# Attention heads of block 1 with the values stationary: probabilities turned by products with diagonals of inverse row sums

## The reference

```python
def first_block(x, w_in, ..., w_out, norm_mix, norm_ffn, w_ff1, w_ff2):
    for l in range(DEPTH):
        h = rmsnorm(x, norm_mix[l])
        proj = jnp.einsum('bsd,de->bse', h, w_in[l])
        ...
        y_m = mlstm(qk[..., :M_WIDTH], qk[..., M_WIDTH:], m_v, m_o, ...)
        y_b = moba(b_q, b_k, b_v, ...)
        y_n = nsa(n_q, n_kc, n_vc, n_ks, n_vs, n_kw, n_vw, n_g, ...)
        mix = jnp.concatenate([y_m, y_b, y_n], axis=-1)
        x = x + jnp.einsum('bse,ed->bsd', mix, w_out[l])
        h = rmsnorm(x, norm_ffn[l])
        u = jnp.square(jax.nn.relu(jnp.einsum('bsd,df->bsf', h, w_ff1[l])))
        x = x + jnp.einsum('bsf,fd->bsd', u, w_ff2[l])
# in nsa, for each head:
    return gj[:, 0] * o_c + gj[:, 1] * o_s + gj[:, 2] * o_w
```

## Time and profile before

| | us |
|---|---|
| runs | 1138.59, 1140.25, 1141.14; median 1140.25 |
| the profiled execution | 1139.48 |
| its span | 1137.7 |
| TensorE busy | 1089.9 (96%) |
| VectorE busy | 717.2 (63%) |
| ScalarE busy | 623.3 (55%) |
| GpSimd busy | 57.5 (5%) |
| block 1, layer 0: projection and heads | about 11 to 170 |
| block 1, layer 1: the same | about 346 to 506 |

### The profile page before, as it was taken

How to read it: one execution, slowest core, us unless ns; L and a number is a source line. 1 busy time by engine, 2 the same in 40 slices (tenths; PEclk the granted TensorE clock), 3 DMA queues, 4 the chain that set the end, 5 groups by cost and what they waited for, 6 DMA issues and landing times.

```text
span 1137.7 us, 17472 instructions
## 1 busy us (share of the span) xinstructions
PE 1089.9 (96%) x6848; PEld 952.3 (84%) x6848; DVE 717.2 (63%) x1260; ACT 623.3 (55%) x983; POOL 57.5 (5%) x75
## 2 busy tenths in 40 slices
PE   8989989999999989899999999999999899999997
PEld 6878779899888977779998987798988677989885
DVE  4799577555557898576555556774445657844555
ACT  4555746445545555745454445665657447666562
POOL 0010000000000000100000000004000000040000
PEclk8999999999999999999999999999999999999999
DMA  8753336655666542346656655554453455444441
GB/s 272 236 162 94 111 111 209 198 186 186 185 190 206 181 130 87 118 128 206 187 187 183 195 187 185 168 152 131 120 158 118 129 161 168 149 130 131 147 130 56
DMA packets 89087, 181.17 MB, mean 159 GB/s; under 512 B 8797, under 2 KB 19933, under 8 KB 89005
## 3 DMA queue, kind: packets, MB, share of 16 engines
q1 hardware_dynamic: 87565, 175.79, 49.8%
q10 hardware_dynamic: 1440, 4.26, 1.1%
HBM read 178.98 MB, written 1.05 MB: 158 GB/s over the span
## 4 chain that ended last, share of the span: by engine, by line
PE 73%; DVE 14%; ACT 5%; issue 5%; DMA 2%; POOL 1%; SPq 0%; DVEq 0%; POOLq 0%; ACTq 0%
PE bank L778 21%; PE bank L780 21%; PE bank L779 21%; DVE w_lo L1623 4%; ACT w_hi L1252 2%; DMA raw<-in_w_in 2%; PE bank L855 2%; PE bank L906 1%; DVE xn L1895 1%; DVE vecs L1632 1%; PE bank L953 1%; PE bank L1191 1%; PE bank L962 1%; PE bank L963 1%; PE bank L929 1%
## 5 line engine op out<-in xcount | busy, mean ns | idle before, releaser
L1623 DVE TENSOR_TENSOR w_lo<-raw,w_hi 128x1024 fp32r<-128x1024 f32 (+1 forms) x320 | 389.4, 1220 | 309.2 <-ACT w_hi L1252 305.0
L1252 ACT ACTIVATE w_hi<-raw 128x1024 fp32r<-128x1024 f32 (+1 forms) x320 | 334.8, 1051 | 243.2 <-PE bank L780 219.6
L778 PE MATMUL bank<-h_hi,w_hi 128*128 128x256 f32 x896 | 257.4, 287 | 4.2 <-ACT hid_parts L1391 4.1
L780 PE MATMUL bank<-h_hi,w_lo 128*128 128x256 f32 x896 | 253.3, 283 | 0.0
L779 PE MATMUL bank<-h_lo,w_hi 128*128 128x256 f32 x896 | 253.3, 283 | 0.0
L778 PE MATMUL bank<-w_hi,h_hi 128*128 128x512 f32 (+1 forms) x448 | 182.6, 407 | 5.4 <-DVE h_lo L1642 4.8
L778 PEld LDWEIGHTS bank<-h_hi,w_hi 128*128 128x128 f32 x896 | 170.9, 191 | 8.2 <-issue 7.0
L780 PE MATMUL bank<-w_hi,h_lo 128*128 128x512 f32 (+1 forms) x448 | 176.4, 394 | 0.0
L779 PE MATMUL bank<-w_lo,h_hi 128*128 128x512 f32 (+1 forms) x448 | 176.2, 393 | 0.0
L779 PEld LDWEIGHTS bank<-h_lo,w_hi 128*128 128x128 f32 x896 | 171.0, 191 | 0.5
L780 PEld LDWEIGHTS bank<-h_hi,w_lo 128*128 128x128 f32 x896 | 170.9, 191 | 0.0
(11 more groups left out here) (290 smaller groups left out, 1329.2 us busy)
## 6 DMA issues: line engine op xcount, KB each, us to landing
raw<-in_w_in SPq DMA_DIRECT2D x144, 512.0 KB, 3.8
raw<-in_w_ff SPq DMA_DIRECT2D x128, 512.0 KB, 4.0
raw<-in_w_out SPq DMA_DIRECT2D x40, 512.0 KB, 3.2
raw<-in_w_in SPq DMA_DIRECT2D x8, 404.0 KB, 5.8
xn<-in_cmp_w SPq DMA_DIRECT2D x8, 256.0 KB, 5.0
x_sb<-in_x SPq DMA_DIRECT2D x2, 512.0 KB, 7.5
mix<-in_cmp_w SPq DMA_DIRECT2D x4, 256.0 KB, 4.7
gain<-in_cmp_w SPq DMA_DIRECT2D x4, 256.0 KB, 5.5
```

The lines of the kernel that those rows point to most:

```text
L778: pe.matmul(out_ap, s_hi, m_hi, start=start, stop=False, **kw)
L780: return pe.matmul(out_ap, s_lo, m_hi, start=False, stop=stop, **kw)
L1252: act.activation(slot(w_hi, u), slot(raw, u), ACT.Copy).then_inc(hi_ready, 1)
L1623: dve.tensor_tensor(slot(w_lo, u), slot(raw, u), slot(w_hi, u).bitcast(F32), ALU.subtract)\
```

## The change

The twelve heads go in six pairs, two heads from start to end (the nsa heads are listed so that a pair takes two heads of the same branch). Each pair gets a stage D on VectorE: reciprocals of its row sums, from head 4 on times the gate, and four 128x128 diagonals of these (row_scale, in the place of vecs). T is then a full product of a block of probabilities with a diagonal, which turns and scales at once. In V the values are stationary, 64 columns for each of two heads side by side, and the turned probabilities move (256 and 128 columns), so the result has features in the partitions. It is split directly into mixT_hi and mixT_lo (mix_rows). The epilogue, mix_turn 2 and 3 and the addition of cmp_o on VectorE go; cmp_o accumulates into the same bank. Some steps move: cmp 0 and 1 to p = 13 and 14, cmp_kT to 20, cmp_s and cmp_soft to 22, cmp_pT to 25, mLSTM scores 3 to 27 and values 3 to 28, ff_params with two casts to 29, three memsets to GpSimd at the start. mlstm_end goes in two halves of two heads each; its last two wide products become four products of 128x128 for each half. Banks change, and some one-element copies that served as signals are gone, since their readers wait for the bank's own semaphore.

```diff
-        start = [13, 14, 15, 16] + list(range(18, 26))
+        start = [13, 15, 18, 20, 22, 24]
         def heads1(p):
-            for stage, lag in (("V", 4), ("T", 2), ("E", 1), ("S", 0)):
+            name = ("att1", l)
+            for c, first in enumerate(start):
+                if first + (4 if c == 5 else 5) == p:
+                    if c in (0, 2):
+                        use((*name, "O", c // 2), 7)
+                    if c in (1, 5):
+                        done((*name, "O", c // 4))
+                    step(*name, "V", 2 * c)
+                    if c in (1, 5):
+                        step("mix_rows", l, c // 4)
+            for h in range(12):
+                c = h // 2
+                if start[c] + 3 + (h % 2 if c < 5 else 0) == p:
+                    use((*name, "T", h), 4 if h == 11 else 6)
+                    step(*name, "T", h)
+            for c, first in enumerate(start):
+                if first + 2 == p:
+                    step(*name, "D", 2 * c)
+            for stage, lag in (("E", 1), ("S", 0)):
                 for h in range(12):
...
+                    if start[h // 2] + lag == p:
+                        head_steps(name, h, stage, None)
...
+                if p == 22:
                     single(0, "cmp_s", l, 0)
                     single(1, "cmp_s", l, 1)
                     step("cmp_soft", l)
-                if p == 21:
-                    single(0, "mix_turn", 0, l, 2)
-                if p == 24:
+                if p == 25:
                     single(3, "cmp_pT", l)
-                if p == 25:
                     m_scores(0, 2)
                 if p == 26:
-                    single(3, "cmp_o", l)
+                    step("cmp_o", l)
...
             if p == 28:
-                m_scores(3, 4)
                 m_values(2, 5)
+                step("mlstm_end", l, 0, 0)
+                m_values(3, 4)
             if p == 29:
-                single(6, "mix_turn", 0, l, 3)
-                m_values(3, 5)
-                step("mlstm_end", l, 0)
+                step("mlstm_end", l, 0, 1)
+                step("mlstm_end", l, 1, 0)
+                if l == 0:
+                    step("ff_params")
             if p == 30:
-                step("mlstm_end", l, 1)
+                single(7, "mix_turn", 0, l, 0)
+                step("mlstm_end", l, 1, 1)
             if p == 31:
-                single(7, "mix_turn", 0, l, 0)
                 single(5, "mix_turn", 0, l, 1)
...
+            def value_pair(l, h):
+                for c in range(2):
+                    drained(pe, ("att1", l, "T", h + c))
+                group = ("att1", l, "O", h // 4 if h < 4 else 1)
...
+                for i in range(NT):
+                    for c in range(2):
+                        v = heads_of("att1", l)[h + c][3](i)
+                        weight = probsT_at("att1", h + c)
+                        mm = pe.matmul(ps[HD * c:HD * c + HD, lo + i * P:lo + T], v, weight[:, i * T:i * T + T - i * P],
+                                       start=first and i == 0, stop=last and i == 1, skip_group_check=True)
...
                     else:
-                        pe.wait_ge(exp_ready, nth_head(kind, l, h))
+                        pe.wait_ge(scale_ready, 6 * l + h // 2 + 1)
...
+                        if kind == "att1":
+                            mm = pe.matmul(ps[:, b * P:(b + 1) * P], block_, row_scale[h // 2 % 2][:, 2 * (h % 2) + (b + 1) // 2, :],
+                                           start=True, stop=True)
+                        else:
+                            mm = pe.transpose(ps[:, b * P:(b + 1) * P], block_, ident)
...
+                def scale_rows(h):
+                    dve.wait_ge(exp_ready, nth_head("att1", l, h + 1))
+                    inv = row_inv[:, 0:2, :]
+                    link(dve.reciprocal(inv, row_sum[:, h // 2 % 2, 0:2, :]))
+                    if h >= 4:
+                        n, branch = divmod(h - 4, 4)
+                        at_gate = 4 * (1 + branch // 2) + 2 * n
+                        tt(inv, inv, n_gate[:, :, at_gate:at_gate + 2].rearrange("p i h -> p h i"), ALU.mult)
+                    dve.tensor_tensor(row_scale[h // 2 % 2], ident.unsqueeze(1).broadcast_to([P, 4, P]),
+                                      inv.rearrange("p h i -> p (h i)").unsqueeze(2).broadcast_to([P, 4, P]), ALU.mult)\
+                        .then_inc(scale_ready, 1)
```

More of the change, by code:

```diff
@@ L296, in hybrid_blocks @@
                 if p == 16:
-                    single(3, "hidden", l)
+                    single(2, "hidden", l)
                 if p == 17:
                     single(3, "turn", l, 2)
-                    single(3, "turn", l, 3)
+                    single(2, "turn", l, 3)
                 if p == 18:
@@ L303, in hybrid_blocks @@
                     single(3, "turn", l, 5)
[L304 to L307, removed]
                 if p == 20:
+                    single(1, "cmp_kT", l)
+                if p == 22:
                     single(0, "cmp_s", l, 0)
@@ L582, in hybrid_blocks @@
         prm_rows = o_tmp[:, 0:2 * P]
+        row_scale = [vecs[:, 1536 * b:1536 * b + 512].rearrange("p (n t) -> p n t", t=P) for b in range(2)]
         ident = const[:, C_ID:C_ID + P]
@@ L1043, in _ @@
                             ps = open_bank(("hidden_parts", l))
-                            pe.wait_ge(blocks_ready, l + 1)
+                            drained(pe, ("turn", l, 4))
                         for a in range(16):
@@ L1417, in _ @@
                         softmax_stage(kind, l, s[2], s[3])
+                    elif kind == "mix_rows":
+                        c = 2 * s[2]
+                        turned(("att1", l, "O", s[2]), mixT1_hi[1][:, c:c + 2, :])
                     elif kind == "mix_turn":
-                        g, c = divmod(2 * s[3], 4)
-                        turned(s, mixT1_hi[g][:, c:c + 2, :])
+                        c = 2 * s[3]
+                        turned(s, mixT1_hi[0][:, c:c + 2, :])
                     elif kind == "square":
@@ L1770, in _ @@
                         residual(s[1:-2], s[-2], s[-1])
-                    elif kind == "params":
+                    elif kind == "ff_params":
                         dve.wait_ge(ident_loaded, 16)
@@ L1956, in _ @@
                             row_max(("att1", l), s[3], C_CAUSAL)
-                        elif s[2] == "V" and s[3] % 4 == 3:
-                            epilogue1(s[3] // 4)
-                    elif kind == "mlstm_end" and s[2] == 0:
-                        for h in range(MH):
+                        elif s[2] == "D":
+                            scale_rows(s[3])
+                    elif kind == "mlstm_end" and s[3] == 0:
+                        r = slice(2 * s[2], 2 * s[2] + 2)
+                        for h in (2 * s[2], 2 * s[2] + 1):
@@ L1977, in _ @@
-                        tt(hn, hn, inv.unsqueeze(3).broadcast_to([P, NT, MH, P]), ALU.mult)
-                        dve.tensor_tensor(mix[:, :, 0:512].rearrange("p i (h d) -> p i h d", d=P), hn, o_gate, ALU.mult)\
-                            .then_inc(mix_ready, 1)
+                        for h in (2 * s[2], 2 * s[2] + 1):
+                            for i in range(NT):
+                                ins = dve.scalar_tensor_tensor(mix[:, i, P * h:P * h + P], h_num[:, i, h, 0:P],
+                                                               m_den[:, i, 4 + h:5 + h], o_gate[:, i, h, :], ALU.mult, ALU.mult)
+                                if h % 2 and i:
+                                    ins.then_inc(mlstm_mixed, 1)
+                                else:
+                                    link(ins)
+                    elif kind == "mix_rows":
+                        c = 2 * s[2]
+                        turned(("att1", l, "O", s[2]), mixT1_hi[1][:, c:c + 2, :], mixT1_lo[1][:, c:c + 2, :])
```

170 lines of the change are left out of this document (79 added, 91 removed).

## The result

The changed kernel takes 1150.0 us (median of 4 runs, 1149.1 to 1151.3); the kernel before took 1139.4 in its runs beside them. The ratio is 1.0097, 95% interval 1.0084 to 1.011: slower by 11 us, where 1142.3 and a range of 1135 to 1147 were forecast. The profiled execution took 1151.3, its span is 1149.5.

The account below looks back on a forecast made before the run. VectorE's list was taken to set the pace from 46 to 119 us, TensorE the second stretch. Layer 0 +0.9, layer 1 +2.8 and the slow stretch -1.7 made +2.0 on 1140.25: 1142.3 us, range 1135 to 1147.

Parts of the forecast that it names:

- Where VectorE's convolution ends: Last convolution step before the Silu: VectorE's added and removed work moves its end +1.3 us in layer 0, +2.7 in layer 1.
- TensorE's waits are free as long as VectorE is behind: From 46 to 119 us VectorE sets the pace, so TensorE's waits there are slack; removing them counts nothing.
- the 0.95 is absorbed: Silu's 0.95 us delay behind the convolution vanishes; w_lo of unit 27 starts +0.35 us in layer 0, +1.75 in layer 1.
- count nothing either: Ahead of the Silu, new waits of the turns of heads 0, 4 and 6 for D, up to 3 us each, cost nothing.
- second stretch: From unit 26's end to the fifth output unit: 26.0 us instead of 28.0, so -2.0 in each layer.
- D behind the split of unit 27: D of heads 8 and 9 stands behind w_lo on VectorE, adding 1.13 us before the turn that needs it.
- 2.2, 0.33 and 0.2 for unit 26: Layer 0 delays ahead of unit 26: later turn start, its second pass, and cmp_pT moved in; given as +2.9 us.
- The slow stretch at 490.30: Half-clock stretch behind layer 1's output projection loses the 1.3 us wait ahead of it: -1.7 us.
- The value pair: Values of two heads on TensorE take 0.86 us, between 0.66 and 1.31, instead of 1.29; -0.86 for two pairs.
- The turn: Turning one head on TensorE takes two passes per block instead of one: 0.66 us instead of 0.33, +0.33.
- Slower: Rival, chance 0.16: column halves of the value pairs do not overlap and each edge drains; 1145 to 1147 us.
- the waits are real: Rival, chance 0.12: VectorE does not pace before the Silu, so 4.8 us of removed TensorE waits per layer count; 1132 us.

Follow-up runs that it names:

- e10: e9 with VectorE's step D left out too (no reciprocals, no diagonals; division and gates left out of the result): 1128.0 us, ratio 0.9906.
- e6: Changed kernel with cmp_s at p = 20, D of heads 8 and 9 ahead of unit 27's split, cmp_soft at p = 24: 1138.7 us, ratio 0.9999.
- b4: Kernel before the change with each of the 24 turns made twice on TensorE: 1138.6 us, ratio 1.0001.
- b3: Kernel before the change with cmp_soft at p = 24, the turn of p_cmp at 26 and cmp_o at 27: 1145.2 us, ratio 1.0058.
- e1: Changed kernel with one move undone: cmp_kT back at p = 19, cmp_s and cmp_soft back at p = 20: 1145.0 us, ratio 1.0054.
- e5: Changed kernel with the edits of e1 and e3, and the mLSTM's second half ahead of the first mix turn, ff_params behind it: 1137.1 us, ratio 0.9988.
- e3: Changed kernel with D of heads 8 and 9 one p earlier, ahead of the split of unit 27: 1145.9 us, ratio 1.0064.
- e9: e6 with e5's mLSTM end order, and the turns as transpositions (diagonals made but unused): 1134.4 us, ratio 0.9959.

## Why the prediction was wrong

**Where VectorE's convolution ends: right.** +1.3 and +2.7 us were forecast for the two layers, +1.7 and +2.2 were measured (layer 1: 459.94 against 451.71, less the 6.0 that layer 0 had brought); for layer 0 the other traces of the changed order give +0.3 to +1.3. That VectorE's list sets the pace there is shown by e10 and e6, where less VectorE work brings the Silu forward, and b4 fits it. That TensorE's waits are free as long as VectorE is behind holds less far: in the kernel before the margin was about 0.5 us (b3).

**The step that failed** is "after, those exponentials are due earlier than the convolution, since cmp_soft has moved behind them. So the 0.95 is absorbed". On VectorE cmp_soft did move behind the maxima. On ScalarE its exponential moved ahead of the exponentials of heads 8 and 9, because these come one p after their scores. I had followed the moved step on VectorE and on TensorE and not on the third engine that takes part in it. Instead of right behind the convolution the Silu starts 3.13 us after it in both layers, and the w_lo of unit 27 is +3.9 late and not +0.35.

A second sentence fails at the same place: the new waits of the turns for D "count nothing either". e1 shows that, with the move undone, D of heads 6 and 7 holds a turn for 3.23 us, the turn holds a copy on ScalarE and the copy holds the same exponentials, so that the Silu is still 2.3 us late. VectorE's backlog doesn't cover that wait, since ScalarE's list ahead of the Silu hangs on it.

The profiled runs are 11.8 us apart (1151.3 and 1139.5), where 2.0 were forecast. 6.3 of the excess of 9.8 us are these 3.13 us in two layers, 2.6 lie between the Silu and unit 26, and 1.5 in the second stretch; unit 26 itself took 0.9 less than forecast. The moved step costs 5.0 of the 10.6 us lost (e1). The three edits of order in e5 together give 12.9 us, more than was lost, so the loss is one of places in the order.

**D behind the split of unit 27: right in place and in its own size.** +1.1 for each layer was forecast, and unit 26 starts 1.2 and 0.9 us earlier without it (e3). The edit gives 4.1 us for both layers, because half-clock time goes with it. This was not counted: in the change 4.8 us of small products ran at 0.50. (The forecast's 2.2, 0.33 and 0.2 for unit 26 are 2.7 and not the 2.9 that it goes on with, and 4.1 and not 4.3 in layer 1; this changes nothing.)

**The second stretch: too good by half.** 26.0 was forecast, 27.15 and 26.35 were measured. TensorE's work was sized well (24.70 us, forecast 24.7), and the wait for mixT_lo that I kept is gone; but the wait for mix did not shrink to 0.3, it grew to 2.25 us in layer 0 and 1.45 in layer 1. I had the casts, the split and the first turn's mixT_lo ahead of the second half in the order of rows, and priced them at 0.3. The edit of e5 gains 5.1 us for both layers.

**The slow stretch at 490.30** is gone, as forecast: from 490.3 to the first units of the feed-forward part the changed kernel gains 1.6 us.

**The value pair: right.** 0.80 us (0.86 forecast; 1.29 before). By columns 1.31 us lie in it, so the two halves overlap and the gain is 1.6. The Trainium skill, page TensorEngine Tiling (Array Packing), section Theoretical Speedup, gives up to 2 for a dimension of 64 or less, and what its section Key Properties says, that a change of tiling mode drains TensorE, may be the 0.14 us over 0.66; no run here takes the drain apart.

**The turn: right in size, and almost without effect.** It takes 0.67 us (136.10 to 136.77) against 0.33. The Trainium skill, page TensorE: Matmul & The Clock Gate, section Terms, has transposition four times faster for FP32; here it is twice, and the measurement decides.

**The rivals.** None of the four is what came. *Slower* gave 1145 to 1147 for halves that don't overlap, and they do overlap. What comes nearest to *the waits are real* is that one of the new waits was real (that of heads 6 and 7 for D), but it costs time and doesn't save any. The 2.6 us between the Silu and unit 26 and the part of the clock in them were not taken apart.

## What to carry to other kernels

A step that several engines share is moved on each of their lists, and the three lists need not agree on what it passes: write the order around it for every engine, and look for what is queued behind its wait on the one that waits longest. A wait on one engine's list that was harmless two places earlier costs its full length when the next item is the critical one. What an engine waits for just ahead of a chain's end is priced with the half clock that can follow. Two traces can lie over a microsecond apart before the first edited instruction, so read a shift from the last event that both share.

## What the runs showed of the hardware

Waits of TensorE of 3.4 us (the change, ahead of 127.60) and 3.37 us (e9, ahead of 95.17) were each followed by 5.5 to 6.7 us in which TensorE ran at 1.2 GHz. The clock didn't always fall at once: in layer 1 of the change and in e3 the value pair behind such a wait (3.44 and 3.43 us) still ran at full clock (0.88 and 0.80 us to the next start), and most of the turn behind it at 1.2 GHz. Behind the 2.25 us ahead of 162.83 the granted clock was 1.00 up to 172. Two weight blocks of 64 columns with 128 rows each, side by side, gave 0.80 us for 1.31 us of columns. Twice the transpositions of 24 heads, 8 us of TensorE's work, cost at most 1.5 us where another engine sets the pace, in part since less time was spent at 1.2 GHz.
